# Index scores of a sparse-attention kernel: the first head's weighting moved from VectorE to ScalarE

## The reference

```python
s_idx = jnp.einsum('bqhd,bld->bqhl', qi, k_idx)
score = jnp.einsum('bqh,bqhl->bql', wi.astype(jnp.float32),
                   jax.nn.relu(s_idx).astype(jnp.float32))
score = jnp.where(causal[None], score, -jnp.inf)
```

## Time and profile before

| | us |
|---|---|
| median of three runs | 3950.34 |
| the profiled execution | 3951.39 |
| its span, first to last instruction | 3949.3 |
| the score stage, first matmul to VectorE's last instruction | 269.6 to 440.3 |
| busy over the whole span: TensorE | 3468.5 (88%) |
| VectorE | 2108.9 (53%) |
| ScalarE | 2018.6 (51%) |

### The profile page before, as it was taken

How to read it: one execution, slowest core, us unless ns; L and a number is a source line. 1 busy time by engine, 2 the same in 40 slices (tenths; PEclk the granted TensorE clock), 3 DMA queues, 4 the chain that set the end, 5 groups by cost and what they waited for, 6 DMA issues and landing times. The chain is left out here.

```text
span 3949.3 us, 63256 instructions
## 1 busy us (share of the span) xinstructions
PE 3468.5 (88%) x18146; PEld 2506.8 (63%) x18146; DVE 2108.9 (53%) x5803; ACT 2018.6 (51%) x3487; POOL 534.6 (14%) x556
## 2 busy tenths in 40 slices
PE   5668798876999999996985999999988888889799
PEld 3546454455666666664864888889945555555687
DVE  3449799995555555554644000000077777777344
ACT  2438689963777777775224111111065666666222
POOL 2000155101111111110110111111030000000011
PEclk8889899986999999998997999999999999999898
DMA  6762477663322322323542222222231111110342
GB/s 209 158 161 43 152 227 230 188 207 94 85 82 77 81 78 81 81 82 127 162 138 88 76 70 74 75 69 67 65 99 41 46 46 46 46 46 27 116 141 97
DMA packets 399606, 402.71 MB, mean 102 GB/s; under 512 B 73376, under 2 KB 324672, under 8 KB 398656
## 3 DMA queue, kind: packets, MB, share of 16 engines
q1 hardware_dynamic: 390704, 400.49, 34.1%
q10 hardware_dynamic: 8720, 0.03, 0.1%
HBM read 254.66 MB, written 145.75 MB: 101 GB/s over the span
## 5 line engine op out<-in xcount | busy, mean ns | idle before, releaser
L1244 DVE CUSTOM_DVE_ANT_0 a_att_sb_lg<-a_att_ps_s,mask 128x512 f32<-128x512 f32 (+3 forms) x512 | 302.2, 595 | 236.4 <-PE a_att_ps_s L1138 196.8
L393 ACT ACTIVATE b_qkgv_sb_o_lo<-b_qkgv_ps_acc 128x512 f32<-128x512 f32 x128 | 76.6, 598 | 638.5 <-PE b_qkgv_ps_acc L376 473.3
L1275 DVE MEMSET b_att_sb_mx<- 128x256 f32 x1 | 0.3, 272 | 722.5 <-PEq L88 722.5
L1318 ACT ACTIVATE a_att_sb_pT<-a_att_ps_t 128x512 f32<-128x512 f32 (+3 forms) x640 | 315.7, 530 | 105.8 <-PE a_att_ps_t L1154 99.0
L1246 DVE TENSOR_SCALAR_CACHE_REDUCE b_att_sb_lg<-b_att_ps_s 128x512 f32<-128x512 f32 (+3 forms) x512 | 289.8, 591 | 137.1 <-PE b_att_ps_s L1143 126.9
L1310 ACT ACTIVATE b_att_sb_lg<-b_att_sb_lg,b_att_sb_negm 128x384 f32<-128x384 f32 (+15 forms) x256 | 305.7, 1198 | 111.0 <-DVE b_att_sb_negm L1252 110.5
L1310 ACT ACTIVATE a_att_sb_lg<-a_att_sb_lg,a_att_sb_negm 128x384 f32<-128x384 f32 (+15 forms) x256 | 307.3, 1201 | 78.0 <-DVE a_att_sb_negm L1252 78.0
L1154 PE MATMUL a_att_ps_t<-ident,a_att_sb_lg 128*128 128x128 f32 x2176 | 339.7, 279 | 0.0
L1143 PE MATMUL b_att_ps_s<-b_att_sb_k,b_att_sb_q 64*128 64x512 f32 (+3 forms) x1280 | 324.3, 593 | 14.1 <-DMA b_att_sb_k<-scratch_kT 9.8
L1137 PE MATMUL a_att_ps_s<-a_att_sb_k,a_att_sb_q 128*128 128x512 f32 (+3 forms) x640 | 287.2, 449 | 48.1 <-DMA a_att_sb_k<-scratch_kT 28.6
L1672 DVE TENSOR_SCALAR_CACHE_REDUCE mask<-scores,threshold_bits 128x384 bf16<-128x384 f32 (+8 forms) x288 | 322.6, 1187 | 1.2
(11 more groups left out here) (272 smaller groups left out, 6868.0 us busy)
## 6 DMA issues: line engine op xcount, KB each, us to landing
select_sb_w_gate<-in_a_w_in SPq DMA_DIRECT2D x32, 512.0 KB, 4.8
mask_sb_mod_w<-in_mod_w SPq DMA_DIRECT2D x16, 1024.0 KB, 6.5
a_att_sb_q<-scratch_qT SPq DMA_DIRECT2D x128, 128.0 KB
a_att_sb_q<-scratch_qT SPq DMA_DIRECT2D x256, 64.0 KB
a_att_sb_k<-scratch_kT SPq DMA_DIRECT2D x64, 256.0 KB
b_qkgv_sb_w<-in_b_w_in SPq DMA_DIRECT2D x32, 512.0 KB
front_sb_mod_w<-in_mod_w SPq DMA_DIRECT2D x8, 1024.0 KB, 6.8
scratch_hT<-front_sb_h SPq DMA_DIRECT2D x32, 256.0 KB, 3.6
```

The lines of the kernel that those rows point to most:

```text
L1244: x = nc.vector.tensor_tensor_reduce(out, src, tab, 1.0, 2 * NEG, sign, ALU.max, top[:, col:col + 1])
L1318: nc.scalar.activation(pT[:, r % 2, a:z, c:c + P], t_ps[:, n % TR, 0:z - a], ACT.Copy).then_inc(t_left, 1)
```

## The change

ScalarE gets a second instruction for head 0: it copies the rectified tile into `scores` with a per-partition scale, the weight. VectorE's multiplication at head 0 goes; it only adds the heads 1 to 7. A new semaphore, `begun`, counts the copies. Where ScalarE waited for VectorE to be done with the unit two back, it waits for its own copy if that unit was a head 0. VectorE's addition at head 1 waits for the copy.

```diff
@@ -1362,11 +1362,12 @@
-        k_in, scored, relued, summed, hidden, causal_step = (
-            st.sem(n) for n in ("k_in", "scored", "relued", "summed", "hidden", "causal_step"))
+        k_in, scored, relued, begun, summed, hidden, causal_step = (
+            st.sem(n) for n in ("k_in", "scored", "relued", "begun", "summed", "hidden", "causal_step"))
         q_in = [st.sem(f"q_in{u}") for u in range(4)]
 
         units = [(i + e, SELECTING[i + e], h) for i in range(0, len(SELECTING), 2) for h in range(IH) for e in range(2)]
+        added = [sum(h > 0 for _, _, h in units[:n]) for n in range(len(units) + 1)]
@@ -1414,10 +1415,17 @@
             for n, (i, b, h) in enumerate(units):
+                N = (b + 1) * P
                 act.wait_ge(scored, n + 1)
                 if n >= 2:
-                    act.wait_ge(summed, n - 1)
-                nc.scalar.activation(relu[:, n % 2, 0:(b + 1) * P], s_ps[:, n % 2, 0:(b + 1) * P], ACT.Relu).then_inc(relued, 1)
+                    if units[n - 2][2]:
+                        act.wait_ge(summed, added[n - 1])
+                    else:
+                        act.wait_ge(begun, units[n - 2][0] + 1)
+                nc.scalar.activation(relu[:, n % 2, 0:N], s_ps[:, n % 2, 0:N], ACT.Relu).then_inc(relued, 1)
+                if h == 0:
+                    act.wait_ge(relued, n + 1)
+                    nc.scalar.activation(scores[:, mask_offset(b):mask_offset(b) + N], relu[:, n % 2, 0:N], ACT.Copy, scale=widx[:, b, 0:1]).then_inc(begun, 1)
@@ -1425,18 +1433,19 @@
-                dve.wait_ge(summed, n + 1)
+                dve.wait_ge(summed, added[n + 1])
                 nc.vector.tensor_tensor(scores[:, z - P:z], scores[:, z - P:z], causal[:], ALU.add).then_inc(hidden, 1)
...
-                dve.wait_ge(relued, n + 1)
-                if h == 0:
-                    nc.vector.tensor_scalar(out, relu[:, n % 2, 0:N], w, 0.0, ALU.mult, ALU.add).then_inc(summed, 1)
-                else:
-                    dve.wait_ge(summed, n - 1)
+                if h:
+                    dve.wait_ge(relued, n + 1)
+                    if h == 1:
+                        dve.wait_ge(begun, i + 1)
+                    else:
+                        dve.wait_ge(summed, added[n - 1])
                     nc.vector.scalar_tensor_tensor(out, relu[:, n % 2, 0:N], w, out, ALU.mult, ALU.add).then_inc(summed, 1)
```

## The result

The changed kernel took 3962.08 us (median of 22 runs), the kernel before 3949.96 us (22 runs beside them). The ratio is 1.0028, 95% interval 1.0020 to 1.0037: 11.1 us slower (7.9 to 14.6), the medians 12.1 us apart. The forecast was 3962.8 us, +12.5. A second set of twelve runs gave 1.0021 (1.0007 to 1.0035).

What follows compares the result with a forecast made beforehand. ScalarE's queue was taken to bound head 0, VectorE heads 1 to 7. Copies 16.8, waits +0.24, overlaps -0.6, filled gaps -2.27, returned idle -1.80, first pair 0.1: +12.5 on 3950.34, 3962.8 us; range 3956 to 3971.

Steps and rivals of the forecast that it cites:

- The two regimes: Score stage: VectorE is the bound at heads 1 to 7, ScalarE at head 0.
- nothing for the removed work: Head 0: VectorE's 14 multiplications, 11.9 us, lie under longer rectifications, so removing them gains nothing.
- The copies: ScalarE at head 0: 14 added copies, 18.1 us together; the 12 that matter cost 16.8 us.
- The own waits: ScalarE at head 0: each copy waits for the rectification just before it, 0.02 us each, +0.24 for 12.
- The overlap: ScalarE's queue: a next activation starts some 0.1 us before its predecessor ends, -0.6 us over six pairs.
- The last pair: Last two tiles: first tile's head 1 starts 3.51 us later; 0.19 comes back, leaving 3.3 us.
- the sum: Score stage: 16.8 + 0.24 - 0.6 - 2.27 - 1.80 gives +12.4 us for six later pairs, 0.1 for the first.
- Behind the stage: After the score stage: nothing softens the loss, as all engines meet at its end before next loads.
- Busy sums: Score stage: only engines' busy totals count, 149.5 against 156.6 us, so -7.1 us, 3943 us; 7 in 100.
- Clock: TensorE's clock falls at the new pauses ahead of pairs, +7.5 us more, 3970 us; 7 in 100.
- Tables: ScalarE: copy and rectification need different tables, 28 loads of 1.28 us add 36 us, 3999 us; 1 in 100.
- Change held by another wait: Head 0: for instance ScalarE held until VectorE has also finished, at most +1 us; 2 in 100.

Runs made afterwards that it cites:

- `drop_only`: Kernel before with VectorE's 14 head-0 multiplications cut to one column each, sums otherwise starting from GpSimd's zeros; stage 171.0 us, ratio 1.0002.
- `after`: The changed kernel itself, first profile, against the kernel before; median 3962.08 us, ratio 1.0028.
- `after_again`: The changed kernel run and profiled once more, nothing altered; score stage 182.7 us again.
- `copy_twice`: Changed kernel with each head-0 copy made once more into a spare tile; one run 3983.8 us, stage 206.9 us.
- `after_three`: Changed kernel with three buffers for the rectified tile in place of two; stage 176.9 us, ratio 1.0016.
- `after_four`: Changed kernel with four buffers for the rectified tile in place of two; stage 176.5 us, ratio 1.0016.
- both parts alone: Kernel before with only ScalarE's copies added: stage 182.8 us, ratio 1.0044; with only VectorE's head-0 multiplications cut: 171.0 us, 1.0002.

## Why the prediction was right

**The two regimes, and nothing for the removed work.** Right, and shown by `drop_only`, not only argued. Reading only the busy sums would have given -7 us.

**The copies.** 18.1 us expected from the counting activations, 18.4 measured; 1.90 and 2.01 us for the two largest, where 1.88 and 1.99 were taken (2.01 is a hair above the "1.9 to 2.0" beyond which the prediction called itself wrong).

The Trainium skill, page "ScalarE: Activation LUTs", section "What ACT_TABLE_LOAD costs", adds about 93 ns for each per-partition operand to 186 ns + 0.833 ns per column. For 14 copies of 17024 columns that is an estimate of 18.1 us; this case's 18.4 is within 2%. For the 12 copies that matter, 16128 columns, the Trainium skill's figures there give an estimate of 16.8 us, the prediction's own term; that they would make the sum about 0.2 us lower was miscalculated.

**The own waits.** 0.02 us taken each; measured 414.48 - (412.66 + 1.78) = 0.04. The guess was close, but the -0.08 at its lower end rested on a misread row: VectorE's mask addition at 404.90. By the code it waits for the last addition of its own tile, the one ahead of that at 402.90, which was long done, so it shows only how a next instruction overlaps, not an own wait. The overlap was 0.1 us as taken (416.38 to 416.28).

**The last pair.** Expected +3.51 us at head 1 of the first tile, and +3.3 at that of the second. Measured from the first rectification to head 1: 421.86 - 412.66 = 9.20 us, before 408.74 - 403.06 = 5.68: +3.52. By the ends of the pairs the loss came in steps of 0.0, 0.8, 1.3, 1.7, 2.2, 2.7 and 3.2 us, 12.0 in all, where the sum had 0.1 for the first and 12.4 for the other six. Over these six, head 1 came 14.4 us later behind the first rectification, where the sum had 14.2 (16.8 + 0.24 - 0.6 - 2.27); what VectorE got back inside the pairs was 2.35 us where 1.80 were taken. There, and in the 0.1 of the first pair, lies the half microsecond: the terms were each off by a few tenths and partly cancelled. VectorE's idle time ahead of head 1, expected to be about 7 us at the last pair, was 6.87.

**Behind the stage.** Nothing softened it, as said. One small thing was added that no step had: 0.98 us between VectorE's last instruction and its first of the next stage, where it was 0.57 before. It is 0.98 in all five profiles of kernels in which VectorE has no multiplication at head 0 at all (`after`, `after_again`, `copy_twice`, `after_three`, `after_four`) and 0.57 in the other seven, so it comes with the change. Its cause was not tried.

**The size against the bound.** The stage's 12.0 us is what tests the sum; that the medians also lie within 1 us of the forecast is partly luck, as the interval is 7.9 to 14.6. 12.5 us lay just above the 0.3% that separates slower from the same, and the measured 1.0028 lies just below; the chances, 59 to 39, said that it would be close, not on which side.

**The rivals.** Busy sums: refuted by both parts alone. Clock: didn't happen (1.00 in the new pauses), as the stretch of the second attention had suggested; with the second copy it did, and cost about 7.2 us. That this is close to the 7.5 put on it is partly chance: the pairs took from 0 (the fifth) to 2.4 us (the sixth), not one such round each. Tables: no load stands between copy and rectification. Change held by another wait: no.

**Where my reasoning was off** is in an experiment, not in the forecast: of `after_four` I expected 10 us back and got 6, and only about 1 of these belongs to the change's loss, since the kernel before gains 5 by a third buffer as well. The prediction's own remark that two-deep buffers let VectorE make up nothing is true but not the point: with a third buffer TensorE and ScalarE save up 1.7 us by the start of the last pair and nothing by that of the small ones, and the kernel before would have had that lead too.

## What to carry to other kernels

An engine with the largest busy sum is not the bound in every part of a stage: before moving work off it, find at that very instruction who waited for whom. Here the multiplication waited for ScalarE, so moving it onto ScalarE lengthened the one queue that set the pace, and what it freed was idle time. Where two engines alternate as the bound and a short ring of buffers joins them, a further buffer may do what shifting work was meant to do: one more gave 5 us, the shift cost 12. And a variant of the changed kernel says what holds its loss only beside the same variant of the kernel before: the third buffer's 6 us looked like half of the loss, and 5 of them were no part of it.

## What the runs showed of the hardware

TensorE's pauses at the start of each pair, up to 1.69 us, left its clock at the upper level, though it was busy only 6.98 of 10.4 us at the last. With a second copy in a loop otherwise the same it came back at the lower level, a 512-column matmul at 0.79 us in place of 0.50, after 3.48 us at the last pair and after only 1.43 us at the second. The length of a pause alone doesn't tell whether the clock falls. A delay on another engine can thus cost more than its own length once it starves TensorE: 16 us of copies cost 24, 7 of the 8 us beyond them in the pairs where the clock fell.

The mean granted clock of the changed kernel's runs ranged from 0.935 to 0.942, and its time by 28 us with it, more than twice the effect measured here. Effects of this size need a stage's own length beside the medians.
